# A fused encoder block on one core: three mixing stages for six levels, and a reordered opening

## The reference

```
mod = silu(c) @ ada_w + ada_b            # six vectors: shift, scale, gate, twice
h = rmsnorm(x) * (1 + scale_a) + shift_a
proj = h @ w_in                           # 1024 -> 4104
mixed = token_mix(proj)                   # 4 retention heads, 4 gated DeltaNet heads
x = x + gate_a * (mixed @ w_out)
h = rmsnorm(x) * (1 + scale_m) + shift_m
x = x + gate_m * (relu(h @ w_ff1)**2 @ w_ff2)   # 1024 -> 4096 -> 1024
return rmsnorm(x)
```

## Time and profile before

| | |
|---|---|
| median of 3 runs | 2903.96 us (2897.76 to 2906.05) |
| the profiled execution, its own time | 2899.68 us |
| its span, first to last instruction | 2897.9 us |
| mean granted TensorE clock | 0.995 |
| TensorE busy | 2816.1 us, 97% |
| TensorE's weight loads | 2363.9 us, 82% |
| VectorE busy | 1344.6 us, 46% |
| ScalarE busy | 1167.7 us, 40% |
| GpSimd busy | 1764.0 us, 61% |
| HBM traffic | 107 GB/s over the span |

### The profile page before, as it was taken

The page is one execution under the profiler, slowest core; times in us unless marked ns, Lnnn a source line. Parts: engine busy times, 40 slices in busy tenths (PEclk is TensorE's granted clock), DMA queues, the critical chain, the costliest instruction groups (busy, mean ns, idle before and its releaser), DMA issues.

```text
span 2897.9 us, 38068 instructions
## 1 busy us (share of the span) xinstructions
PE 2816.1 (97%) x14376; PEld 2363.9 (82%) x14376; DVE 1344.6 (46%) x1880; ACT 1167.7 (40%) x2033; POOL 1764.0 (61%) x1331
## 2 busy tenths in 40 slices
PE   3899999999999999999999999999999999999998
PEld 2788888888888888888888888888888888888886
DVE  5656555454546546453535425544353443322133
ACT  2534343453334434353444434353333434443332
POOL 5656554676657756575656756666565657566553
PEclk9999999999999999999999999999999999999999
DMA  6334344432333323322232323423222224233342
GB/s 258 108 133 137 118 136 153 133 114 92 101 114 119 99 69 119 119 84 84 79 115 91 109 80 97 143 74 91 77 86 82 84 81 135 87 102 95 95 124 88
DMA packets 98102, 311.89 MB, mean 108 GB/s; under 512 B 11520, under 2 KB 11520, under 8 KB 95872
## 3 DMA queue, kind: packets, MB, share of 16 engines
q1 hardware_dynamic: 67248, 247.05, 27.4%
q10 hardware_dynamic: 30672, 62.40, 6.5%
HBM read 285.29 MB, written 24.12 MB: 107 GB/s over the span
## 4 chain that ended last, share of the span: by engine, by line
PE 88%; DVE 5%; POOL 2%; issue 2%; ACT 1%; DMA 1%; ACTq 0%; SPq 0%; POOLq 0%; DVEq 0%
PE acc L482 24%; PE acc L484 24%; PE acc L483 24%; PE pm L518 8%; PE pm L523 3%; DVE mixing L1197 1%; DMA x<-in_xT 1%; POOL w L1610 1%; POOL mT L1619 1%; POOL row L1692 1%; PE pm L614 1%; PE pm L532 1%; PE pm L619 0%; PE pm L645 0%; DMA raw<-in_w_all 0%
## 5 line engine op out<-in xcount | busy, mean ns | idle before, releaser
L1610 POOL TENSOR_TENSOR w<-raw,w 128x512 fp32r<-128x512 f32 x832 | 1130.1, 1361 | 957.6 <-ACT w L717 956.7
L717 ACT ACTIVATE w<-raw 128x512 fp32r<-128x512 f32 x832 | 521.6, 629 | 730.1 <-PE acc L484 673.3
L482 PE MATMUL acc<-mT,w 128*128 128x512 f32 x1536 | 626.6, 408 | 14.5 <-POOL w L1610 8.3
L484 PE MATMUL acc<-mT,w 128*128 128x512 f32 x1536 | 602.5, 392 | 0.0
L483 PE MATMUL acc<-mT,w 128*128 128x512 f32 x1536 | 600.4, 391 | 0.0
L482 PE MATMUL acc<-hid,w 128*128 128x512 f32 x864 | 352.6, 408 | 2.6 <-DVE ffs L1401 1.4
L482 PEld LDWEIGHTS acc<-mT,w 128*128 128x128 f32 x1536 | 290.3, 189 | 72.2 <-POOL w L1610 10.5
L484 PEld LDWEIGHTS acc<-mT,w 128*128 128x128 f32 x1536 | 289.3, 188 | 63.5
L484 PE MATMUL acc<-hid,w 128*128 128x512 f32 x864 | 338.6, 392 | 0.0
L483 PE MATMUL acc<-hid,w 128*128 128x512 f32 x864 | 337.7, 391 | 0.0
L483 PEld LDWEIGHTS acc<-mT,w 128*128 128x128 f32 x1536 | 290.8, 189 | 52.9 <-issue 1.0
(11 more groups left out here) (224 smaller groups left out, 3837.4 us busy)
## 6 DMA issues: line engine op xcount, KB each, us to landing
raw<-in_w_all SPq DMA_DIRECT2D x416, 512.0 KB, 3.6
ada_late<-in_ada_w SPq DMA_DIRECT2D x32, 512.0 KB, 5.0
xr<-in_xT ACTq DMA_DIRECT2D x48, 256.0 KB, 3.2
mixing<-in_ada_w SPq DMA_DIRECT2D x8, 1024.0 KB, 9.8
proj_kept<-ffs ACTq DMA_DIRECT2D x32, 256.0 KB, 2.3
out<-io ACTq DMA_DIRECT2D x32, 256.0 KB, 2.5
mixed_kept<-mixing ACTq DMA_DIRECT2D x28, 256.0 KB, 2.2
xr<-mixed_kept ACTq DMA_DIRECT2D x28, 256.0 KB, 2.7
```

The source lines that it names most:

```text
L482: e.matmul(bank, whi, x[:, 0, :], start=first, stop=False)
L484: m = e.matmul(bank, wlo, x[:, 0, :], start=False, stop=last)
L717: e.activation(w2[:, 0, local % HALVES, :], raw[:, tile % NRAW, local % 2 * NT:(local % 2 + 1) * NT], ACT.Copy).then_inc(S["w_hi"], 1)
L1610: e.tensor_tensor(w2[:, 1, local % HALVES, :], raw[:, tile % NRAW, local % 2 * NT:(local % 2 + 1) * NT], w2[:, 0, local % HALVES, :].bitca ...
```

## The change

In the mixing: the six levels become three stages. A stage takes two levels at once by three products on TensorE: y1 = x U, Q1 = U - y1; y2 = x Q1, Q2 = U - y2; y3 = Q2 x (in the last stage x Q2), and T = T - y3 (in the last stage U = U - y3). Both Q are made by VectorE. The k that enters the products is no longer normalised: k k^T is taken from k itself, and the factors go into beta (`bnk`), into v (`vnorm`) and stay out of the rest; the transposes of the normalised k and its copy go away. The cumulative decays, their exponentials and their negatives are made once for the four units of a block. In the opening: VectorE adds the squares of x; piece 0 of ada_w goes through TensorE (`first_piece`); SyncE, ScalarE and GpSimd take the orders shown; the copies of B1, GA, B2, GM and WF go away, these being read where they lie.

The diff, cut to its core, in the order of the file: names and buffers, and SyncE; TensorE; ScalarE; VectorE; GpSimd. Counts of waits that only follow the new numbers are left out.

```diff
-LEVELS = 7
+STAGES = 3
...
-        (yk, sqk, sqq, gs, LT, orr, th, swp,
-         yq, yv, knat, kT, vnat, Dm, attn, og) = (mixing[:, i, :] for i in range(16))
-        T, U, X, Lm, bD = yk, yv, sqk, sqq, gs
+        (T, sqk, sqq, gs, LT, orr, th, swp,
+         yq, yv, knat, yk, vnat, Dm, attn, og) = (mixing[:, i, :] for i in range(16))
+        U, X, Lm, bD, Q = yv, sqk, sqq, gs, og
...
             def ada_load(k):
-                if k >= 4:
-                    e.wait_ge(S["mod_used"], k - 3)
+                if k == 4:
+                    e.wait_ge(S["piece_used"], 1)
+                elif k > 4:
+                    e.wait_ge(S["mod_used"], k - 4)
...
-                    for j, mask in enumerate((upper, strict, ones)):
-                        m = e.matmul(bB[:, 4 * j:4 * j + 4], mask, decay_of(n), start=True, stop=True)
-                    m.then_inc(S["gc_out"], 1)
+                    if u == 0:
+                        for j, mask in enumerate((upper, strict, ones)):
+                            m = e.matmul(bB[:, 16 * j:16 * j + 16], mask, gb[:, n // HEADS % 2, :, 0:SUB], start=True, stop=True)
+                        m.then_inc(S["gc_out"], 1)
...
-                if s == 15:
-                    e.wait_ge(S["k_nat"], n + 1)
-                    turn(bE, knat).then_inc(S["kt_out"], 1)
...
                 if s == 17:
-                    e.wait_ge(S["kt_ready"], n + 1)
...
-                    four(bB, kT, kT)
-                    four(bF, kT, yq).then_inc(S["kk_out"], 1)
+                    four(bB, yk, yk)
+                    four(bF, yk, yq).then_inc(S["kk_out"], 1)
...
-                if 22 <= s <= 42 and s % 4 == 2:
...
-                        turn(bF, T).then_inc(S["t_turned"], 1)
-                    four(bE, Lm, T).then_inc(S["x_out"], 1)
-                if 24 <= s <= 44 and s % 4 == 0:
...
-                    if l < LEVELS - 1:
-                        four(bB, U, X).then_inc(S["y_out"], 1)
-                    else:
-                        four(bF, X, U).then_inc(S["y_out"], 1)
+                st, step = divmod(s - 22, 8)
+                if 0 <= st < STAGES and step == 0:
...
+                        e.wait_ge(S["t_next"], (STAGES - 1) * n + st)
+                        turn(bF, T).then_inc(S["t_turned"], 1)
+                    four(bE, Lm, T).then_inc(S["x_out"], 1)
+                if 0 <= st < STAGES and step == 2:
...
+                    four(bB, X, U).then_inc(S["y_out"], 1)
+                if 0 <= st < STAGES and step == 4:
+                    e.wait_ge(S["q_ready"], 2 * STAGES * n + 2 * st + 1)
+                    four(bB, X, Q).then_inc(S["y_out"], 1)
+                if 0 <= st < STAGES and step == 6:
+                    e.wait_ge(S["q_ready"], 2 * STAGES * n + 2 * st + 2)
+                    if st < STAGES - 1:
+                        four(bF, Q, X).then_inc(S["y_out"], 1)
                     else:
+                        four(bF, X, Q).then_inc(S["y_out"], 1)
...
+            def first_piece(bank):
+
+                e.wait_ge(S["ada0"], 16)
+                e.wait_ge(S["silu_v"], 4)
+                for j in range(16):
+                    m = e.matmul(bank[:, 2 * j:2 * j + 2], ada_slot(0)[:, j * P:(j + 1) * P], scol[:, 0:2], start=True,
+                                 stop=True)
+                m.then_inc(S["piece_used"], 1)
+
+            first_piece(bD_)
             e.wait_ge(S["const_in"], 32)
             column_sums(0, bB)
...
-                    e.activation(vnat, bB, ACT.Copy, scale=0.5).then_inc(S["v_nat"], 1)
...
-                if s == 15:
-                    e.wait_ge(S["kt_out"], n + 1)
-                    e.activation(kT, bE, ACT.Copy).then_inc(S["kt_ready"], 1)
...
+            hi(3)
             for i in range(UNIT):
-                hi(2 * i + 3)
                 hi(2 * i + 4)
                 evac(i)
+                if i < UNIT - 1:
+                    hi(2 * i + 5)
...
-                if i >= 5:
-                    for j in (2 * (i - 5), 2 * (i - 5) + 1):
-                        next_h(1, j)
-                        if j < 4:
-                            ring_load("xn", 1, j + 4)
+            for j in (0, 1):
+                next_h(1, j)
+                ring_load("xn", 1, j + 4)
...
-                    if n == 0 and s < 2:
-                        next_h(1, 6 + s)
+                    if n == 0 and s < 6:
+                        next_h(1, 2 + s)
+                        if s < 2:
+                            ring_load("xn", 1, 6 + s)
...
-                if s == 55:
-                    twice_silu(S["tanh_k"], m, yk, tanh_at[GK], conv_at[GK], S["y_k"])
...
-                    e.tensor_tensor(by_sub(knat), by_sub(bE), over_tokens(nk), ALU.mult).then_inc(S["k_nat"], 1)
+                    e.scalar_tensor_tensor(out=vnorm, in0=ssk, scalar=0.5, in1=nk, op0=ALU.mult,
+                                           op1=ALU.mult).then_inc(S["ss_steps"], 1)
+                    e.tensor_tensor(nk2, nk, nk, ALU.mult).then_inc(S["ss_steps"], 1)
+                    e.wait_ge(S["ss_steps"], 7 * n + 4)
+                    e.tensor_tensor(bnk, nk2, beta_of(n), ALU.mult).then_inc(S["ss_steps"], 1)
+                    e.tensor_tensor(by_sub(vnat), by_sub(bB), over_tokens(vnorm), ALU.mult).then_inc(S["v_nat"], 1)
...
                 if s == 14:
+                    e.tensor_tensor(by_sub(knat), by_sub(bE), over_tokens(grown(n, 1)), ALU.mult).then_inc(S["k_nat"], 1)
...
+                if 0 <= st < STAGES and step in (2, 4):
+                    e.wait_ge(S["y_out"], 3 * STAGES * n + 3 * st + step // 2)
...
+                    e.tensor_tensor(Q, U, bB, ALU.subtract).then_inc(S["q_ready"], 1)
+                if 0 <= st < STAGES and step == 6:
+                    e.wait_ge(S["y_out"], 3 * STAGES * n + 3 * st + 3)
...
-                        e.tensor_tensor(T, T, bB, ALU.subtract).then_inc(S["t_next"], 1)
+                        e.tensor_tensor(T, T, bF, ALU.subtract).then_inc(S["t_next"], 1)
...
-            for k in range(KT):
+            for k in range(1, KT):
+                for j in {1: (1, 2, 3, 4), 2: (5, 6), 3: (7,)}.get(k, ()):
+                    add_square(0, j)
                 first_sum(k)
+                if k == 3:
+                    e.wait_ge(S["piece_used"], 1)
+                    e.tensor_tensor(adab[:, 0:16], bD_[:, 0:32:2], adab[:, 0:16], ALU.add).then_inc(S["mod_steps"], 1)
...
-            e.tensor_copy(B1, mod[:, 0:8]).then_inc(S["mod_steps"], 1)
...
-                if s == 11:
+                if s == 13:
                     e.wait_ge(S["d_mask"], n + 1)
-                    e.tensor_tensor(by_sub(bD), by_sub(Dm), over_tokens(beta_of(n)), ALU.mult).then_inc(S["beta_d"], 1)
+                    e.wait_ge(S["ss_steps"], 7 * n + 5)
+                    e.tensor_tensor(by_sub(bD), by_sub(Dm), over_tokens(bnk), ALU.mult).then_inc(S["beta_d"], 1)
...
-                if 18 <= s <= 38 and s % 4 == 2:
+                if s in (18, 26, 34):
...
-                if s == 41:
...
-                    e.tensor_tensor(by_sub(knat), by_sub(knat), over_tokens(eg[:, 4:8]), ALU.mult).then_inc(S["kd_ready"], 1)
...
-            for j in range(1, KT):
-                e.wait_ge(S["sq_ready"], j + 1)
-                if j > 1:
-                    e.wait_ge(S["sq_added"], j - 1)
-                e.tensor_tensor(sqrow, sqrow, io[:, j % 2, :], ALU.add).then_inc(S["sq_added"], 1)
```

More of the change, by code:

```diff
@@ L296, in build @@
         wgs = sb("wgs", [P, 2, KT, 8], F32R)
+        eg = sb("egs", [P, 3, HEADS, SUB])
+        negc = sb("negcs", [P, HEADS, SUB])
         ident, ones, upper, strict = (consts[:, i, :] for i in range(4))
         mod = ab[:, 0:48]
-        A1, B1, GA, A2, B2, GM, WF = (ab[:, 48 + i * KT:48 + (i + 1) * KT] for i in range(7))
+        A1, A2 = (ab[:, 48 + i * KT:48 + (i + 1) * KT] for i in range(2))
+        B1, GA, B2, GM = (mod[:, i * KT:(i + 1) * KT] for i in (0, 2, 3, 5))
         ccol = ab[:, 104:112]
@@ L307, in build @@
         negA = small[:, 44:48]
-        eg = small[:, 48:60]
-        negc = small[:, 60:64]
         ssk, ssq, nk, nq = (small[:, 64 + 4 * i:68 + 4 * i] for i in range(4))
@@ L314, in build @@
         gbt = small[:, 192:208]
+        vnorm, nk2, bnk = (small[:, 216 + 4 * i:220 + 4 * i] for i in range(3))
         scol = small[:, 208:216]
@@ L613, in mix @@
                     e.wait_ge(S["g_state"], SUB * n + t)
-                    e.matmul(sub(bB, t), sub(kT, t), s_gdn(n), start=True, stop=True).then_inc(S["ks_out"], 1)
+                    e.matmul(sub(bB, t), sub(yk, t), s_gdn(n), start=True, stop=True).then_inc(S["ks_out"], 1)
                     e.matmul(sub(bF, t), sub(yq, t), s_gdn(n), start=True, stop=True)
@@ L1517, in _ @@
                 front(0, s)
+            for s in range(47, SLOTS):
+                front(0, s)
             keep_row(h1, bD_)
@@ L1520, in _ @@
             next_normed(1, 1)
[L1521 to L1528 removed]
             e.wait_ge(S["lmask_in"], 16)
```

(15 more changed lines are left out.)

146 lines of the change are left out of this document (67 added, 79 removed).

## The result

The changed kernel takes 2854.63 us (median of 4 runs, 2852.43 to 2856.99) against 2902.69 for the kernel before in the same comparison: ratio 0.9835, 95% interval 0.9823 to 0.9847. It is faster by 48 us. The forecast was 2850, range 2838 to 2866. The profiled execution took 2852.43 us with a span of 2850.6; the one before took 2899.68 with 2897.9, so on that scale, where the sum was 53.7, it gained 47.3.

A forecast was written before the change was run, and what follows sets the result against it. TensorE, matmul-busy 97% of the span, was taken as the bound. 35.6 + 4.3 - 2 + 6.0 + 9.8 = 53.7 us off 2899.68 gave 2846.0, on the median's level 2850; 8-in-10 range 2838 to 2866.

The forecast's parts named there:

- Mixing, TensorE's work: Mixing on TensorE: 64 fewer transposes, 28.8 us, and 12 fewer sets of small decay products, 7.1 us; taken as 35.6 us.
- Rival 3: TensorE's removed mixing work is worth only 82%: 6.4 us less gain, 2857 us; chance 0.06.
- Waits that go: Mixing: TensorE's waits for the normalised k and for ScalarE's copy of it disappear, 4.3 us gained.
- waits that are added: Mixing: three more VectorE round trips a unit for the Q's cost 2 us, bounds 0 to 14.
- Rivals 4 and 5: Mixing's Q's: half of 48 round trips wait 1 us, 2874, chance 0.07; or TensorE stands, 2932 or above, chance 0.03.
- The opening: Up to the first dense matmul: last sums end at 37.9 against 43.03, B1 copy goes; 6.0 us gained, ends 1.5 and 8.
- the B1 copy: Opening, VectorE: removing this copy ahead of the first dense matmul gains its 1.21 us.
- Rival 2: Opening does not start sooner, as piece 0's slot is freed 5.7 us later: gain 1.5 or less, 2855; chance 0.08.
- The stalls: Three TensorE stalls from 107 to 128 us: 7.95 plus 3.1 of clock less 1.3 gives 9.8 us, ends 0 and 11.
- 1.3 us are given back: Window 0: the exponential of slot 8 stands behind moved input pieces in ScalarE, costing TensorE 1.3 us.
- costed at nothing since neither end of the old chain made TensorE wait: Mixing, slot 17: later v and scores' mask cost nothing; without cover, 1 us a unit in the first block.
- Rival 1: Stalls only move: window 0 waits for the second block's input, 9.8 us lost, 2860; chance 0.12.

The follow-up runs named there:

- after: The changed kernel as in the diff, against the kernel before: 2854.63 us median of 4 runs; its profiled execution took 2852.43 us.
- squares_pool: Changed kernel with the seven adds of squares in the opening given back to GpSimd: 2852.68 us.
- no_piece: Changed kernel with piece 0 of ada_w summed on VectorE again, its TensorE matmuls taken away: 2854.22 us.
- before: The kernel without the change: 2902.69 us median in the comparison; its profiled execution took 2899.68 us.
- before_mask: The kernel before the change, with the scores' mask made first in VectorE's slot 13: 2902.39 us.
- best: Changed kernel with the mask first in VectorE's slot 13 and GpSimd's third weight part behind the first input's low parts: 2844.39 us, ratio 0.9799 to the kernel before.
- mask_first: Changed kernel with the scores' mask made first in VectorE's slot 13: 2843.91 us.
- h_split: Changed kernel with the last two of six second-block input parts moved from window 0's first slots to slots 9 and 12: 2855.26 us.

## Why the prediction was right, and which of its terms were off

**Mixing, TensorE's work: right, a little small.** 64 transposes at 0.45 to 0.47 are 28.8 to 29.9 and 12 sets of small products at 0.68 are 8.2, 37 to 38 for the 35.6. The set was priced 0.59 from the row between its first start and the next dense one; 0.09 more lies behind it. Rival 3, 82% of the price, is out: in steps 1408 to 1504, without a stall, three transposes cost 1.41 us where the full price is 1.35 and 82% of it 1.11; over the span 48 of them cost 22.2 for 21.6 and 17.7. The rule of the Trainium skill (Perfetto Trace Analysis, Identifying the Most-Contended Engine), by which busy time is a poor measure of TensorE's headroom, would have given the lower number; the even starts of the earlier trace rows were the better reading here.

**Waits that go and waits that are added.** Both waits of the earlier trace rows that I let go are gone. The Q's cost nothing visible where I took 2 us of bounds 0 to 14: the wait for the unit's last update fell from 1.8 to 1.2 us. Rivals 4 and 5 are out.

**The opening: the right place, the B1 copy mis-sized.** The last sums end at 38.03, forecast 37.9; piece 4 is there by 26.90, forecast 26.6. Rival 2 is out. The term that failed is the copy of B1, 1.21 us, which I let go. Its duration was not the copy's. In the earlier trace rows and in after the first small operation of VectorE with no operand in PSUM that meets GpSimd's weight part is held for 1.2 us, whichever it is: with the copy gone, it is A1 (1.21, up to 46.54, where GpSimd's third part has just ended at 46.51), and with the weight part moved A1 takes 0.17. The Trainium skill (SBUF — State Buffer, Who interferes with whom) says that a VectorE instruction with both inputs in SBUF contends with a GpSimd instruction that reads SBUF, by an exclusive lock. The trace agrees for A1, 1.21 us beside a part of 1.24 and 0.17 without it. And the reason I gave for the 5.1 us, that GpSimd's adds are what is late, was half: either edit alone gives most of it, 38.22 - 34.32 = 3.9 us with piece 0 on TensorE and about 4.75 with the squares on VectorE.

**The stalls: their removal right, what they give back not.** Up to step 77 the whole forecast is 17.05 and the trace has 17.03; the closeness is luck, 0.9 too much for the opening and 0.9 too little for the tiles. The term of 9.8 is what was wrong: with the order of the parts undone (experiment 2), the order is worth 11.7 us at step 77 and 5.5 at step 160. The step that failed is "1.3 us are given back", and with it the mask "costed at nothing since neither end of the old chain made TensorE wait". Window 0 has 6.7 us of waits (0.92, 1.78 and 3.99), and behind the last of them the granted clock is 0.52 from 133.75 to 137.00, 1.6 us. Before, the clock had its full rate from step 77 on (1.00 from 132.04 to 137.00), and the only wait of these steps was one of 0.6, which after has too, at 0.41. Rival 1 was half right: the stalls moved in part, but mostly to the mask and not to the second block's input.

I had named the mask's place and its price without cover, 1 us a unit in the first block; it was 4.0 in the first, 0.6 in the next three, and 0.85 twice later. Two things were left out. With the stalls gone TensorE is 17.0 us earlier at step 77, while the mask, behind VectorE's chain (late ada_w sums, a power on GpSimd, v), is only 9.2 earlier (132.93 for 142.08). And a small operation of this chain takes 1.22 us beside a weight part (line 1276, 129.97 to 131.19), as A1 does; that it is held in the same way is read from the times, no run moved this part:
```profile
129.90 1.28 POOL L1636 TENSOR_TENSOR w<-raw,w 128x512 fp32r<-128x512 f32 x1
```
The exponential, which I had late by 1.3, is late by 1.8, and ScalarE's parts of the input end at 121.2, forecast 121. With the transposes' 1.8 us on the other side, less than 1 us of window 0 stays unsplit.

**The sum.** 53.7 less 0.9 (opening), less 7.5 (waits for the mask), less some 3 (1.6 of clock in window 0, and 1.4 by which the waits ahead of the mask's exceed the 1.3), plus 0.9 (tiles), plus 2.4 (TensorE's work), plus 2 (no Q waits) is 47.6; measured 47.3. The forecast lay within 5 us of the median because terms missing at the mask and its clock were partly offset by small terms on the other side. Of the missing ones the mask's alone, 6.4 to 8.0, is shown by runs.

## What to carry to other kernels

When a stall is taken away, the engine behind it comes earlier to every later meeting: read the queues of the next window as they would stand with the new arrival time, and put operations that need nothing first in their slot. A duration far above the usual one of a small operation (here 1.21 us for 0.17) can belong to another engine's operation beside it, and then goes to the next operation when the first is deleted. Two edits for one late chain should be tried singly and both undone, as each may give most of the gain.

## What the runs showed that was not expected

One stretch differs by 6 us between kernels whose edits do not touch it (squares_pool, after, no_piece), and by 3 between before and before_mask. From step 352 to 449 (about 394 to 505 us) before took 111.72, after 110.88, squares_pool 107.71, no_piece 114.04 and before_mask 114.87. TensorE never stands idle for over 0.8 us there; between 465 and 485 us it makes runs of 128x2 matmuls (line 656). Two windows of that stretch in squares_pool, after and no_piece:
```profile
470.00:475.00 5.00, 5.00 (x37) 4.61 (x37) 4.35 (x6) 0.63 (x1) 0.55 (x1) 1.00 0.50 163
480.00:485.00 5.00, 5.00 (x26) 4.18 (x26) 1.50 (x3) 2.40 (x6) 1.28 (x1) 1.00 0.50 132
```
```profile
470.00:475.00 5.00, 5.00 (x23) 4.34 (x22) 2.59 (x4) 0.00 (x1) 0.00 (x0) 0.66 0.41 149
480.00:485.00 5.00, 5.00 (x23) 4.16 (x22) 1.50 (x3) 1.45 (x3) 1.28 (x1) 0.84 0.33 105
```
```profile
470.00:475.00 5.00, 5.00 (x17) 4.13 (x17) 1.34 (x2) 0.00 (x0) 0.00 (x0) 0.53 0.22 83
480.00:485.00 5.00, 5.00 (x16) 4.08 (x15) 1.00 (x3) 0.63 (x1) 1.28 (x1) 0.51 0.35 105
```
The granted clock there is 1.00, 0.66 and 0.84, and 0.53 and 0.51, that is full time at 2.4 GHz, part of it, and nearly all of it at 1.2 GHz, though TensorE is busy for the whole of each window in all three. Whether the small matmuls or how the stretch is entered decide it was not tried. It is worth 3 us either way, so a single run's whole time says less than its steps do. A second case: steps 928 to 1024 took 80.9 us in some runs and 82.5 in others with the same waits; in after and best the granted clock of 920 to 940 us is 0.91, in mask_first and h_split 1.00. And the five executions of best alone spread over 8 us (2838.91 to 2846.9).
